# Moving twelve merge steps of a dilated attention and giving four weight slices another place

## The chip, the cores and the metric

The kernel runs on one core of a Trainium2 chip. A core has five engines with a queue of instructions each: PE (TensorE, matrix products into PSUM), DVE (VectorE), ACT (ScalarE), POOL (GpSimd) and SP (SyncE, which here issues the DMAs). They wait for each other by semaphores alone. The metric is the device time of one execution in microseconds (us).

## The reference

One decoder layer on x of 1024 rows by 1024 columns, all in float32. A single projection feeds three attention branches: A (three head groups with dilations 1, 4 and 16, merged per position by their softmax denominators), B (sliding window, eight query heads that share two key heads, with sinks) and M (four heads against 256 memory rows). Then come gates, an output projection and a feed-forward part with a short convolution. Cut to what the change touches:

```python
def dilated_mixture_attn(qkv_a, positions, q_gain, k_gain):
    for gi, (window, dil) in enumerate(A_GROUPS):
        ...
        o, lse = banded_attn(to_residue(q, dil)[:, :, None], to_residue(k, dil),
                             to_residue(v, dil), window // dil)
        outs.append(from_residue(o[:, :, 0], dil))
        lses.append(from_residue(lse[:, :, 0], dil))
    w = jax.nn.softmax(jnp.stack(lses), axis=0)
    o = jnp.einsum('gbshd,gbsh->bshd', jnp.stack(outs), w.astype(qkv_a.dtype))

def memory_attn(mq, mem, mem_gain, w_kv, q_gain, k_gain):
    ...
    q = rmsnorm(mq.reshape(b, s, M_HEADS, M_HEAD_DIM), q_gain)
    sc = jnp.einsum('bshd,bmhd->bhsm', q, mk).astype(jnp.float32) * (M_HEAD_DIM ** -0.5)
```

## The kernel before

The first part of the kernel, `input_projections`, is a chain of 44 jobs: a job projects one tile of 128 rows of the normalised input by one stage's weights. The stages are A with dilation 1 (jobs 0 to 7), the memory's keys and values (8 to 11), A with dilation 4 (12 to 19), A with dilation 16 (20 to 27), B (28 to 35) and M (36 to 43). Every job is cut into eight steps k = 0 to 7, and (j, k) is step k of job j. Each engine runs through the same double loop in its own queue; the order within a step is that in which the code is written. The attention of job j is done in the steps of job j + 2 (`LAG`): scores on PE, minima of the scores on DVE, exponentials on ACT, transposes of them on PE, products with the values on PE.

*What belongs to a projection.* q and k of job j come out of PSUM in (j+1, 0) by `normalise` on DVE (L1018, L1023, L1025), are multiplied by gains and rotated on POOL (L721 to L737), and are transposed on PE by `turn` in step 5 or 6 of job j+1 (L1345) and, for B, the key once more in step 7 (L1342). `turn` waits until POOL is done, and the second one also until ACT has copied q out of the bank (`copy_q`, L838). `sum_squares` (L999, DVE) stands at the start of the next job, in front of POOL's power (L712), on which `normalise` waits.

*The weights.* Every stage has eight slices, numbered n = 0 to 55 over all stages; those of M are 48 to 55. SP loads slice n (`load_slice`), ACT rounds it to its high part (L799, `cast_slice`), DVE subtracts (L513, `w_low`) to make the low part. The high part has one place for each k, so slice n can be cast only when the last job of the stage before has used slice n - 8. For M the casts of 48 to 52 stand in steps 2 to 6 of job 35, those of 53 to 55 at the start of job 36, in ACT's queue ahead of the copies and exponentials of (36, 0). `raw_place` says where a raw slice lies: M's slices rotate over three places of the buffer `w_raw`, and a load waits (`raw_before`) for the low part of the slice that lay there.

*The merge of A.* The outputs of the three dilations lie in rows 0 to 5 of `attn_out`, one row for each group g and pair of heads. Twelve merge steps m = 0 to 11 (`merge_use`, DVE) multiply them by factors and add them up: m // 6 is the pair of heads, (m // 2) % 3 the group, m % 2 the half. A step of group 0 is one instruction (L1156), one of group 1 or 2 is a product (L1166) and a sum (L1168). `MERGE_AT` lists the job and step of each; `merge_from` is 30. The factors come by DMA into two buffers, `load_factors(q)` for steps 2q and 2q + 1, each once the buffer's last use is over (`factor_used`).

*The late factors.* B's factors are finished in job 38: `late_gaps` (L1128) at the end of job 37, `late_factors` (L1134, L1135, DVE) in (38, 2), and `turn_late` (L1401), a transpose on PE in (38, 4), which waits for them:

```python
                if j == late_from + 1 and k == 4:
                    turn_late()
```

In the trace below job 33 begins on PE near 397.5 us, job 35 near 428.4, job 36 at 445.5, job 37 at 461.3, job 38 at 474.2 and job 39 at 484.2.

Of the kernel before, what the change touches and what calls it, by code (L numbers as in the profile page):

```python
# [68 lines left out]
def half_of(row, h):  # L69
    return 4 + 2 * row + h, 1  # L70


def whole(row):
    return 4 + 2 * row, 2
# [3 lines left out]
RAW_PLACES = ([W0, W1] + [half_of(r, h) for r in (6, 7, 8, 9) for h in range(2)] +  # L78
              [W0, W1] + [half_of(r, h) for r in (6, 7) for h in range(2)] +
              [whole(8), whole(9), W0, W1, whole(6), whole(7), W0, W1] +  # L80
              [whole(6), whole(7), W0, W1] * 4)


def raw_place(n):

    return RAW_PLACES[n - 8] if n < 48 else (n % 3, 1)


def raw_group(n):

    if n < 8:
        return 2 + n
    first = raw_place(n)[0]
    if n >= 48:
        return 7 + first
    return first // 2 if first < 4 else 2 + first - 16


def raw_before(n):

    def pieces(m):
        if m < 8:
            return set()
        first, pieces = raw_place(m)
        if m >= 48:
            return {0, 1, 2, 3}
        return set(range(first, first + pieces))

    def shared(m):
        return raw_group(m) == raw_group(n) or (pieces(m) & pieces(n) and not (m >= 48 and n >= 48))  # L110
    return next((m for m in range(n - 1, -1, -1) if shared(m)), None)


def raw_uses(n):
    return sum(raw_group(m) == raw_group(n) for m in range(n + 1))
# [50 lines left out]
def at(do, step, *more):  # L166
    if 0 <= step < len(STEPS) and STEPS[step] is not None:
        do(STEPS[step], *more)
# [64 lines left out]
def layer(nc, x, mem, positions, attn_norm, w_in, a_q_norm, a_k_norm, b_q_norm, b_k_norm, b_sinks,  # L233
# [14 lines left out]
    with ExitStack() as whole:  # L248
# [34 lines left out]
        with ExitStack() as middle:  # L283
# [26 lines left out]
            with ExitStack() as combining:  # L310
# [5 lines left out]
        ahead = Ahead(ffn_area, f_hi, plain_lo, f_in, blocks, sem("first_hi_done"), sem("first_lo_done"))  # L316

        input_projections(nc, x_t, mem_t, positions, attn_norm, w_in, a_q_norm, a_k_norm, b_q_norm,
                          b_k_norm, b_sinks, mem_norm, w_mem_kv, m_q_norm, m_k_norm, w_gate, w_raw, first_gate,
                          first_gate_in, stats_dram, factor_dram, late_dram, ps, act_hi, act_lo, ident, ident_ready, half_power, attn_out,  # L320
# [34 lines left out]
def input_projections(nc, x_t, mem_t, positions, attn_norm, w_in, a_q_norm, a_k_norm, b_q_norm, b_k_norm,  # L355
# [8 lines left out]
    with ExitStack() as ctx:  # L364
# [3 lines left out]
        def sem(name):  # L368
            return ctx.enter_context(nc.semaphore(name))
# [65 lines left out]
        group_added = sem("group_added")  # L435
# [11 lines left out]
        def x_half(n, h):  # L447
# [6 lines left out]
        last_job_of = {s: max(j for j in range(NJ) if JOBS[j][0] == s) for s in range(len(STAGES))}  # L454
        merge_from = next(j for j in range(NJ) if KIND[j] == "B") + 2

        MERGE_AT = [(merge_from + d, k) for d, k in ((2, 0), (2, 4), (3, 4), (4, 4), (5, 4), (6, 4), (7, 4),
                                                     (8, 1), (8, 5), (8, 7), (9, 1), (9, 5))]
        LATE_AT = [(merge_from + d, k) for d in (10, 11, 12, 13) for k in (2, 6)]
        late_from = last_job_of[5] + LAG  # L460

# [7 lines left out]
        def raw(n):  # L469
            if n < 8:  # L470
                return w_first[:, n, :]
            first, pieces = raw_place(n)
            if n >= 48:
                return w_raw[:].rearrange("p a n -> p (a n)")[:, 512 * first:512 * first + 512]
            if first < 4:
                return w_raw[:, first // 2, :]
            return attn_out[:, (first - 4) // 2, 512 * (first % 2):512 * (first % 2 + pieces)]
# [7 lines left out]
        def x_split(eng, n):  # L485

            even = sum(x_low_on_pool(m) for m in range(n))
            if even:
                eng.wait_ge(x_lo_pool, even)
            eng.wait_ge(x_lo_dve, n - even)  # L490
# [80 lines left out]
        def _(sp):  # L571
            def load_x(n):
                sp.dma_start(x_slot[n], x_t[n] if n < 8 else mem_t[n - 8]).then_inc(x_in[X_GROUP[n]], 16)

            def load_slice(n):
                kind, _, _, col, na, nb, _ = STAGES[n // 8]
                src = w_mem_kv if kind in ("memk", "memv") else w_in
                k = n % 8
                if raw_before(n) is not None:
                    w_split(sp, raw_before(n))  # L580
                sp.dma_start(raw(n)[:, 0:na + nb],
                             src[0, k * P:(k + 1) * P, col:col + na + nb]).then_inc(raw_in[raw_group(n)], 16)
# [22 lines left out]
            def reorder_stats():  # L605

                sp.wait_ge(exp_done, 2 * pairs_before(last_job_of[3] + 1))
                sp.dma_start(stats_dram[0].rearrange("(t p) c -> p t c", p=P), stats[:, 0]).then_inc(stats_out, 16)
                for b in range(2):
                    sp.dma_start(stats_dram[1].rearrange("(b i r) c -> b i r c", b=2, r=4)[b],  # L610
                                 stats[:, 1].rearrange("p (r b) c -> p b r c", b=2)[:, b]).then_inc(stats_out, 16)
                sp.wait_ge(stats_out, 48)
                for g in range(2):
                    sp.dma_start(stats[:, g], stats_dram[g].rearrange("(p t) c -> p t c", t=8)).then_inc(stats_in, 16)

            def store_factors():

                sp.wait_ge(factors_ready, 1)
                sp.dma_start(factor_dram.rearrange("r (p t) -> p r t", t=8),
                             merge["f"][:].rearrange("p (r t) -> p r t", t=8)).then_inc(factors_out, 16)  # L620
                sp.wait_ge(factors_out, 16)

            def load_factors(q):

                pair, g = q // 3, q % 3
                if q >= 2:
                    sp.wait_ge(factor_used, 2 * (q - 1))
                for e in range(2):
                    sp.dma_start(factor_rows[64 * e:64 * e + 64, q % 2, :],
                                 factor_dram[4 * g + 2 * pair + e].partition_broadcast(64)).then_inc(factor_in[q % 2], 16)  # L630
# [9 lines left out]
            for n in range(8, 8 * len(STAGES)):  # L640
                if n == 8 * 5:
                    reorder_stats()
                if n == 8 * 6:
                    store_factors()
                    load_factors(0)
                    load_factors(1)
                if n in (8 * 6 + 3, 8 * 6 + 5):
                    load_factors(2 if n == 8 * 6 + 3 else 3)
                if n == 8 + 2:
                    x_split(sp, 2)  # L650
                    for m in (8, 9):
                        load_x(m)
                if n in (10, 12, 14, 16):
                    x_split(sp, n // 2)
                load_slice(n)
# [271 lines left out]
        def _(dve):  # L927
# [221 lines left out]
            def merge_use(m):  # L1149

                pair, g, half = merge_batch(m)
                dve.wait_ge(factor_in[(m // 2) % 2], 32 * (m // 4 + 1))
                dst = attn_out[:, pair, half * 512:(half + 1) * 512]
                rows = factor_rows[:, (m // 2) % 2, half * 512:(half + 1) * 512]
                if g == 0:
                    dve.tensor_tensor(dst, rows, dst, ALU.mult).then_inc(factor_used, 1)  # L1156
                    dve.wait_ge(factor_used, m + 1)
                    return
                src = attn_out[:, 2 * g + pair, :]
                if g == 1:  # L1160
                    src = src.rearrange("p (r b i) -> p b i r", r=4, b=2)[:, half]
                    rows, dst = (a.rearrange("p (i r) -> p i r", r=4) for a in (rows, dst))
                else:
                    src = src.rearrange("p (t i) -> p i t", t=8)[:, half * 64:(half + 1) * 64]
                    rows, dst = (a.rearrange("p (i t) -> p i t", t=8) for a in (rows, dst))
                dve.tensor_tensor(src, rows, src, ALU.mult).then_inc(factor_used, 1)  # L1166
                dve.wait_ge(factor_used, m + 1)
                dve.tensor_tensor(dst, dst, src, ALU.add).then_inc(group_added, 1)  # L1168
                dve.wait_ge(group_added, 4 * pair + 2 * (g - 1) + half + 1)
# [18 lines left out]
            for j in range(NJ + LAG + 1):  # L1188
# [24 lines left out]
                for k in range(8):  # L1213
                    if k in step_slices(j):
# [4 lines left out]
                        at(copy_out, n - 2)  # L1219
                    if (j, k) in MERGE_AT:  # L1220
                        merge_use(MERGE_AT.index((j, k)))
                    if (j, k) in LATE_AT:
# [36 lines left out]
        def _(pe):  # L1259
# [26 lines left out]
            def project(j, part, k):  # L1286
                s, t = JOBS[j]
                kind, order, _, _, na, nb, tiles = STAGES[s]
                n = 8 * s + k
                if part == "a" and k == 0:  # L1290
# [1965 lines left out]
```

## Time and profile before

| | us |
|---|---|
| median of 3 runs (lowest, highest) | 1643.06 (1641.81, 1645.39) |
| the profiled execution, its own time | 1643.44 |
| its span, first to last instruction | 1641.5 |
| PE busy | 1604.5 |
| DVE busy | 1034.5 |
| POOL busy | 903.6 |
| ACT busy | 706.5 |

The span is what the trace covers; the execution took 1.9 us more than it. Busy times are sums over instructions. A matrix product's end is modelled, and its duration overlaps with the next one's start, so starts are compared rather than durations.

### The profile page before, as it was taken

How to read it: one execution, taken by the hardware profiler on the slowest of the kernel's cores; microseconds unless marked ns; L12 is line 12 of the kernel's file. 1: busy time of each engine (PE TensorE's matmuls, PEld its weight loads, DVE VectorE, ACT ScalarE, POOL GpSimd, SP SyncE). 2: the span in 40 equal slices, each digit the busy share in tenths (PEclk: the TensorE clock that was granted, in tenths of full speed). 3: DMA queues.
4: the chain of work that ended last, by engine and by line, in shares of the span. 5: the costliest groups of instructions: out<-in, count | busy, mean ns of one | idle time of the engine just before them, and what ended most of it. 6: DMA issues, size and time to landing. Idle time of an engine off the chain costs nothing.

```text
span 1641.5 us, 22736 instructions
## 1 busy us (share of the span) xinstructions
PE 1604.5 (98%) x8387; PEld 1322.6 (81%) x8387; DVE 1034.5 (63%) x1479; ACT 706.5 (43%) x1253; POOL 903.6 (55%) x680
## 2 busy tenths in 40 slices
PE   7999999999999999999999999999999999999999
PEld 6887878878878788888888887878888888888887
DVE  6555242345666593223655257988888888889896
ACT  5555565545554434334312223443343344454442
POOL 4643656644322297776345566989999999400000
PEclk9999999999999999999999999999999999999999
DMA  6113011002121323332555711322222222496253
GB/s 228 40 62 106 1 40 43 17 24 60 46 53 39 89 86 112 121 120 80 147 164 156 251 51 52 90 90 78 77 77 80 88 85 95 160 348 236 90 166 136
DMA packets 145865, 167.63 MB, mean 102 GB/s; under 512 B 16852, under 2 KB 97500, under 8 KB 145756
## 3 DMA queue, kind: packets, MB, share of 16 engines
q1 hardware_dynamic: 145324, 166.17, 31.5%
q8 instruction: 68, 1.11, 0.3%
q14 instruction: 41, 0.34, 0.1%
q10 hardware_dynamic: 432, 0.01, 0.0%
HBM read 133.50 MB, written 32.65 MB: 101 GB/s over the span
## 4 chain that ended last, share of the span: by engine, by line
PE 62%; POOL 2%; DVE 1%; ACT 0%; issue 0%; POOLq 0%; ACTq 0%
PE ps L3121 25%; PE ps L3222 13%; PE ps L2201 11%; PE ps L2241 7%; PE ps L2257 5%; POOL f_lo L1928 1%; PE ps L2192 1%; PE ps L2250 0%; POOL ffn_area L1940 0%; POOL ffn_area L1938 0%; POOL ffn_area L1941 0%; POOL ffn_area L1943 0%; DVE t_all L2881 0%; DVE ffn_area L2165 0%; POOL f_lo L2854 0%
## 5 line engine op out<-in xcount | busy, mean ns | idle before, releaser
L2854 POOL TENSOR_TENSOR f_lo<-ffn_area,f_hi 128x1024 fp32r<-128x1024 f32 (+1 forms) x83 | 198.9, 2416 | 20.4 <-ACT f_hi L2727 20.4
L3121 PE MATMUL ps<-t_all,f_hi 128*128 128x512 f32 x528 | 164.0, 392 | 2.0 <-DVE t_all L2881 1.6
L2727 ACT ACTIVATE f_hi<-ffn_area 128x1024 fp32r<-128x1024 f32 x85 | 80.2, 946 | 174.2 <-PE ps L3121 162.9
L3222 PE MATMUL ps<-attn_lo 128*128 128x512 f32 x624 | 143.7, 389 | 0.0
L3222 PEld LDWEIGHTS ps<-attn_lo 128*128 128x128 f32 x624 | 117.2, 188 | 24.4
L3121 PE MATMUL ps<-act_hi,f_hi 128*128 128x512 f32 x336 | 132.8, 395 | 1.3 <-POOL f_lo L2854 1.3
L1928 POOL TENSOR_TENSOR f_lo<-ffn_area,f_hi 128x1024 fp32r<-128x1024 f32 (+1 forms) x42 | 98.2, 2341 | 63.5 <-ACT f_hi L1772 63.5
L3121 PE MATMUL ps<-act_hi,f_lo 128*128 128x512 f32 x336 | 131.8, 392 | 0.0
L3121 PE MATMUL ps<-act_lo,f_hi 128*128 128x512 f32 x336 | 130.8, 389 | 0.0
L1319 PE MATMUL ps<-w_hi,act_hi 128*128 128x512 f32 (+1 forms) x320 | 121.6, 380 | 3.2 <-DVE qk L1025 1.9
L710 POOL TENSOR_SCALAR head_rstd<-head_ss 128x8 f32<-128x8 f32 (+2 forms) x42 | 10.4, 248 | 204.3 <-DVE head_ss L999 204.3
L3121 PEld LDWEIGHTS ps<-t_all,f_hi 128*128 128x128 f32 x528 | 98.9, 188 | 24.5 <-DVE t_all L2881 1.7
L1319 PE MATMUL ps<-w_lo,act_hi 128*128 128x512 f32 (+1 forms) x320 | 111.9, 350 | 0.0
L1319 PE MATMUL ps<-w_hi,act_lo 128*128 128x512 f32 (+1 forms) x320 | 111.7, 349 | 0.0
L3121 PE MATMUL ps<-t_all,f_lo 128*128 128x512 f32 x264 | 103.4, 392 | 0.0
L862 ACT ACTIVATE prob_t<-ps 128x512 f32<-128x512 f32 (+1 forms) x96 | 50.4, 525 | 121.6 <-PE ps L1423 115.4
L721 POOL TENSOR_TENSOR qk<-qk,gains 128x256 f32<-128x256 f32 (+1 forms) x74 | 62.7, 847 | 49.7 <-DVE qk L1023 30.1
L2920 DVE TENSOR_TENSOR attn_out<-attn_out 128x1024 f32<-128x1024 f32 x22 | 68.6, 3118 | 21.4 <-ACT attn_out L2782 21.4
L2257 PE MATMUL ps<-wo,act_hi 128*128 128x512 f32 x256 | 81.0, 397 | 0.0
L3121 PEld LDWEIGHTS ps<-act_hi,f_hi 128*128 128x128 f32 x336 | 63.1, 188 | 15.5 <-POOL f_lo L2854 1.7
L3121 PEld LDWEIGHTS ps<-act_hi,f_lo 128*128 128x128 f32 x336 | 63.0, 188 | 14.9
L2201 PE MATMUL ps<-t_all,f_hi 128*128 128x512 f32 x240 | 74.5, 391 | 0.0
(363 smaller groups left out, 4358.7 us busy)
## 6 DMA issues: line engine op xcount, KB each, us to landing
ffn_area<-in_w_up_dram SPq DMA_DIRECT2D x44, 512.0 KB, 5.2
gate<-gates SPq DMA_DIRECT2D x24, 512.0 KB, 3.6
ffn_area<-in_w_gate_dram SPq DMA_DIRECT2D x23, 512.0 KB, 5.1
z<-attn_out SPq DMA_DIRECT2D x22, 512.0 KB, 2.6
gates<-ffn_area SPq DMA_DIRECT2D x40, 256.0 KB, 2.1
t_raw<-in_w_down_dram SPq DMA_DIRECT2D x34, 256.0 KB, 6.4
attn_out<-in_x_dram SPq DMA_DIRECT2D x16, 512.0 KB, 6.1
f_raw<-in_w_down_dram SPq DMA_DIRECT2D x26, 256.0 KB, 4.7
```

Source lines behind the costliest of these rows:

```text
L721: ins = pool.tensor_tensor(buf[:, h0:h1, :], buf[:, h0:h1, :], gains[:, off:off + dh].unsqueeze(1).to_broadcast([P, h1 - h0, dh]), ALU.mult)
L862: act.activation(prob_t[:, u, :, c0:2, :], prob_turn[:, :, c0:2, :], ACT.Copy).then_inc(prob_copied, 1)
L1319: ins = pe.matmul(dst, lhs, w[:, k, cols], start=(k == 0 and i == 0), stop=(k == 7 and i == 2))
L1928: pool.tensor_tensor(part_place(p, part, f_lo), part_source(p, part), part_place(p, part, f_hi).bitcast(F32), ALU.subtract).then_inc(w_lo_ ...
L2201: ins = pe.matmul(gate_bank(p, i), w[:, slot, cols], a[:, k, :], start=(k == 0 and m == 0), stop=(k == 3 and m == 2))
L2241: ins = pe.matmul(o_bank(at), w[:, i0 + i, :], a[:, t0 + i, HALF[half]], start=(i == 0 and m == 0), stop=(i == tiles - 1 and m == 2))
L2257: ins = pe.matmul(ps[:, n % 4, :], a[:, k, t * P:(t + 1) * P], wo[:, slot, w, :], start=(k == 0 and i == 0), stop=(k == NK - 1 and i == 2))
L2727: act.activation(part_place(p, part, f_hi, first_hi), part_source(p, part), ACT.Copy).then_inc(w_hi_done, 1)
L2854: pool.tensor_tensor(part_place(p, part, f_lo, first_lo), part_source(p, part), part_place(p, part, f_hi, first_hi).bitcast(F32), ALU.subt ...
L2920: dve.tensor_tensor(conv[:, 0, :], conv[:, 0, :], conv[:, 1, :], ALU.mult).then_inc(z_done, 1)
L3121: ins = pe.matmul(out, w, a, start=(start and k == 0 and i == 0), stop=(stop and k == 3 and i == 2))
L3222: ins = pe.matmul(down_bank(i, t), z[a][:, t * P:(t + 1) * P], w[b], start=(k == 0 and n == 0), stop=(k == DEPTH - 1 and n == 2))
```

## The change

Two things are changed. The merge steps take other places: they stand two a job in steps 1 and 5 of jobs 32 to 35, and the last four in (37, 1), (37, 5), (37, 7) and (38, 1). Before, they stood in (32, 0), (32, 4), (33, 4), (34, 4), (35, 4), (36, 4), (37, 4), (38, 1), (38, 5), (38, 7), (39, 1) and (39, 5). And slices 51 to 54 are no longer loaded into `w_raw` but into the halves of rows 2 and 4 of `attn_out`, which hold outputs of pair 0 that are merged after step m = 5; SP waits for that (`group_added`, 4) before it loads them, and both `load_factors(2)` and `(3)` stand ahead of that wait. Slice 55 takes the first place of `w_raw`.

```diff
+LAST_PLACES = [(0, 1), (1, 1), (2, 1)] + [half_of(r, h) for r in (2, 4) for h in range(2)] + [(0, 1)]
+
 def raw_place(n):
-    return RAW_PLACES[n - 8] if n < 48 else (n % 3, 1)
+    return RAW_PLACES[n - 8] if n < 48 else LAST_PLACES[n - 48]
...
     if n >= 48:
-        return 7 + first
+        return {8: 3, 9: 5, 12: 6, 13: 4}[first] if first >= 8 else 7 + first
...
-        if m >= 48:
+        if m >= 48 and first < 4:
             return {0, 1, 2, 3}
...
-        MERGE_AT = [(merge_from + d, k) for d, k in ((2, 0), (2, 4), (3, 4), (4, 4), (5, 4), (6, 4), (7, 4),
-                                                     (8, 1), (8, 5), (8, 7), (9, 1), (9, 5))]
+        MERGE_AT = [(merge_from + d, k) for d, k in ((2, 1), (2, 5), (3, 1), (3, 5), (4, 1), (4, 5), (5, 1), (5, 5),
+                                                     (7, 1), (7, 5), (7, 7), (8, 1))]
...
-            if n >= 48:
+            if n >= 48 and first < 4:
                 return w_raw[:].rearrange("p a n -> p (a n)")[:, 512 * first:512 * first + 512]
...
-                if n in (8 * 6 + 3, 8 * 6 + 5):
-                    load_factors(2 if n == 8 * 6 + 3 else 3)
+                if n == 8 * 6 + 3:
+                    load_factors(2)
+                    load_factors(3)
+                    sp.wait_ge(group_added, 4)
```

SP's queue from the loads of slices 48 to 50 on, before. `factor_rows` are the merge factors, `w_raw<-in_w_in_dram 128x512` is a slice of M:

```order
L581 DMA w_raw<-in_w_in_dram 128x512 [waits w_lo_dve,w_lo_pool] x3
L629 DMA factor_rows<-factors 64x1024 [waits factor_used]
L629 DMA factor_rows<-factors 64x1024
L581 DMA w_raw<-in_w_in_dram 128x512 [waits w_lo_dve,w_lo_pool] x2
L629 DMA factor_rows<-factors 64x1024 [waits factor_used]
L629 DMA factor_rows<-factors 64x1024
L581 DMA w_raw<-in_w_in_dram 128x512 [waits w_lo_dve,w_lo_pool] x3
```

The same place of the changed kernel:

```order
L584 DMA w_raw<-in_w_in_dram 128x512 [waits w_lo_dve,w_lo_pool] x3
L632 DMA factor_rows<-factors 64x1024 [waits factor_used]
L632 DMA factor_rows<-factors 64x1024
L632 DMA factor_rows<-factors 64x1024 [waits factor_used]
L632 DMA factor_rows<-factors 64x1024
L584 DMA attn_out<-in_w_in_dram 128x512 [waits w_lo_dve,w_lo_pool,group_added]
L584 DMA attn_out<-in_w_in_dram 128x512 [waits w_lo_dve,w_lo_pool] x3
L584 DMA w_raw<-in_w_in_dram 128x512 [waits w_lo_dve,w_lo_pool]
```

Slices 51 to 54 come in one run behind a wait for the merge, into `attn_out`; only slice 55 still goes to `w_raw`.

DVE's queue from (37, 5) to `late_factors` in (38, 2), before. `late` is what `late_gaps` and `late_factors` work on, `small<-ps` the minima of M's scores:

```order
L1156 TENSOR_TENSOR attn_out<-factor_rows,attn_out 128x512
L1128 TENSOR_TENSOR late<-late,neg_sink 128x64
L999 TENSOR_REDUCE head_ss<-square 128x4
L1023 TENSOR_TENSOR qk<-ps,head_rstd 128x512
L1058 TENSOR_REDUCE small<-ps 128x4
L1093 COPY attn_out<-ps 128x2x128
L1156 TENSOR_TENSOR attn_out<-factor_rows,attn_out 128x512
L1134 TENSOR_TENSOR late<-late 128x64
L1135 RECIPROCAL late<-late 128x8x8
```

The changed kernel, from the sum that ends merge step 9 (lines are 5 higher):

```order
L1173 TENSOR_TENSOR attn_out<-attn_out 128x512
L1171 TENSOR_TENSOR attn_out<-factor_rows,attn_out 128x64x8
L1173 TENSOR_TENSOR attn_out<-attn_out 128x512
L1133 TENSOR_TENSOR late<-late,neg_sink 128x64
L1004 TENSOR_REDUCE head_ss<-square 128x4
L1028 TENSOR_TENSOR qk<-ps,head_rstd 128x512
L1063 TENSOR_REDUCE small<-ps 128x4
L1098 COPY attn_out<-ps 128x2x128
L1171 TENSOR_TENSOR attn_out<-factor_rows,attn_out 128x64x8
L1173 TENSOR_TENSOR attn_out<-attn_out 128x512
L1139 TENSOR_TENSOR late<-late 128x64
L1140 RECIPROCAL late<-late 128x8x8
```

Ahead of the reciprocal of `late` there stand now three merge steps of a product and a sum (9, 10 and 11; the product of 9 is the row ahead of those shown), where two single products stood (6 and 7).

DVE's queue in job 33, steps 0 and 1, before, from the copy of an output (`attn_out<-ps`) through `normalise` (`qk<-ps,head_rstd`) to the first minima of step 4:

```order
L1093 COPY attn_out<-ps 128x2x128
L1018 TENSOR_TENSOR qk<-ps,head_rstd 128x2x4x64
L1025 TENSOR_TENSOR qk<-ps,head_rstd 128x128
L1069 ISA prob,late<-ps,masks,neg_sink 128x256
L1069 ISA late 128x1
L1069 ISA prob,late<-ps,masks,neg_sink 128x256
L1069 ISA late 128x1
```

The changed kernel:

```order
L1098 COPY attn_out<-ps 128x2x128
L1023 TENSOR_TENSOR qk<-ps,head_rstd 128x2x4x64
L1030 TENSOR_TENSOR qk<-ps,head_rstd 128x128
L1171 TENSOR_TENSOR attn_out<-factor_rows,attn_out 128x128x4
L1173 TENSOR_TENSOR attn_out<-attn_out 128x512
L1074 ISA prob,late<-ps,masks,neg_sink 128x256
L1074 ISA late 128x1
```

Merge step 2 has moved from behind those minima to right behind `normalise`; in job 34 step 4 has moved in the same way.

## Rows read from the trace of the kernel before

**Rows 1.** The page: busy time, share of the span and instructions of each engine.

```profile
PE 1604.5 (98%) x8387; PEld 1322.6 (81%) x8387; DVE 1034.5 (63%) x1479; ACT 706.5 (43%) x1253; POOL 903.6 (55%) x680
```

**Rows 2.** Busy time by stretch: us, then each engine, clock, DMA share, GB/s.

```profile
450.00:500.00 50.00, 47.63 (x335) 38.37 (x334) 33.87 (x73) 25.18 (x72) 12.14 (x18) 1.00 0.20 53
```

**Rows 3.** Timeline of the SP queue: start, us, engine, line, operation, out<-in, count.

```profile
445.01 2.27 SPq L581 DMA_DIRECT2D w_raw<-in_w_in_dram  x3
```

**Rows 4.** Timeline of ACT, same columns; in brackets idle before it and releaser.

```profile
447.76 0.63 ACT L799 ACTIVATE w_hi<-w_raw 128x512 fp32r<-128x512 f32 x1 [0.65 <-DMA w_raw<-in_w_in_dram]
450.22 1.27 ACT L799 ACTIVATE w_hi<-w_raw 128x512 fp32r<-128x512 f32 x2 [1.82 <-DMA w_raw<-in_w_in_dram]
451.39 0.58 ACT L862 ACTIVATE prob_t<-ps 128x512 f32<-128x512 f32 x1
```

**Rows 5.** Timeline of PE in job 36.

```profile
450.60 0.40 PE L1319 MATMUL ps<-w_hi,act_lo 128*128 128x512 f32 x1
452.12 0.63 PE L1392 MATMUL ps<-ident,prob 128*128 128x128 f32 x4 [1.12 <-ACT prob_t L862]
...
453.74 0.39 PE L1319 MATMUL ps<-w_hi,act_lo 128*128 128x512 f32 x1
454.85 0.63 PE L1392 MATMUL ps<-ident,prob 128*128 128x128 f32 x4 [0.73 <-ACT prob_t L862]
...
458.37 0.60 PE L1345 MATMUL ps<-ident,qk 128*128 128x128 f32 x4
...
460.42 0.39 PE L1319 MATMUL ps<-w_hi,act_lo 128*128 128x512 f32 x1
461.17 0.30 PE L1342 MATMUL ps<-ident,qk 128*128 128x128 f32 x1 [0.36 <-issue]
```

**Rows 6.** Timeline of POOL in job 36: gain multiply and end of the rotation.

```profile
453.55 1.82 POOL L721 TENSOR_TENSOR qk<-qk,gains 128x512 f32<-128x512 f32 x2 [3.41 <-DVE qk L1025]
...
456.92 0.52 POOL L737 TENSOR_TENSOR qk<-rope_a,rope_b 128x160 f32<-128x160 f32 x1
```

**Rows 7.** Timeline of DVE in jobs 37 to 39.

```profile
472.38 0.68 DVE L1156 TENSOR_TENSOR attn_out<-factor_rows,attn_out 128x512 f32<-128x512 f32 x1
...
475.64 0.69 DVE L999 TENSOR_REDUCE head_ss<-square 128x4 f32<-128x512 f32 x1 [1.16 <-ACT square L808]
...
479.81 0.68 DVE L1156 TENSOR_TENSOR attn_out<-factor_rows,attn_out 128x512 f32<-128x512 f32 x1
480.53 0.22 DVE L1134 TENSOR_TENSOR late<-late 128x64 f32<-128x64 f32 x1
480.78 0.56 DVE L1135 RECIPROCAL late<-late 128x64 f32<-128x64 f32 x1
...
485.85 1.04 DVE L1166 TENSOR_TENSOR attn_out<-factor_rows,attn_out 128x512 f32<-128x512 f32 x1
...
488.02 0.69 DVE L999 TENSOR_REDUCE head_ss<-square 128x4 f32<-128x512 f32 x1
```

**Rows 8.** Timeline of PE in job 38, at the transpose of the late factors.

```profile
481.31 0.39 PE L1319 MATMUL ps<-w_hi,act_lo 128*128 128x512 f32 x1
481.53 0.27 PE L1401 MATMUL ps<-ident,late 128*64 128x128 f32 x1
```

**Rows 9.** Timeline of DVE: a subtraction in stage one, a minimum in job 33.

```profile
42.92 1.22 DVE L499 TENSOR_TENSOR act_lo<-attn_out,act_hi 128x1024 fp32r<-128x1024 f32 x1
...
407.79 0.48 DVE L1069 CUSTOM_DVE_ANT_1 prob<-ps,masks,neg_sink 128x256 f32<-128x256 f32 x1 [3.83 <-PE ps L1378]
```

**Rows 10.** Timeline of POOL: rotations in stage one and in job 33.

```profile
43.01 1.45 POOL L732 TENSOR_TENSOR rope_a<-qk,rope_cos 128x128 f32<-128x128 f32 x1
...
55.06 0.46 POOL L732 TENSOR_TENSOR rope_a<-qk,rope_cos 128x128 f32<-128x128 f32 x1
...
407.42 0.52 POOL L737 TENSOR_TENSOR qk<-rope_a,rope_b 128x160 f32<-128x160 f32 x1
```

**Rows 11.** Timeline of PE: the transpose of q and k in job 33.

```profile
409.91 0.60 PE L1345 MATMUL ps<-ident,qk 128*128 128x128 f32 x4
```

## The prediction

> **What bounds the kernel now.** I read the page first: PE is busy 1604.5 of 1641.5 us [rows 1], so only what PE waits can be won, and whatever makes it wait is lost. The change touches the stretch of jobs 32 to 39, so the table by stretch comes next: from 450 to 500 us PE is busy 47.63 of 50 us at a granted clock of 1.00 [rows 2], which leaves 2.4 us. Idle time in the records is a lower bound, because modelled ends overlap; in the timeline the reader should compare starts. Two products of 512 columns start 0.22 us apart [rows 8], so a gap above 0.23 behind one is a stall.
>
> In job 36 [rows 5] shows three of them. 450.60 to 452.12 is 1.52 instead of 0.23: 1.29 us of stall, released by ACT's copy. 453.74 to 454.85 gives 0.88 in the same way, again behind ACT's copy. 460.42 to 461.17 gives 0.52, in front of the transpose of B's last key. The first two go back to a DMA. ACT's last two casts start at 450.22 after 1.82 us of waiting for `w_raw`, and the copy that PE needs stands behind them, at 451.39 [rows 4]. SP could issue the last three slices only from 445.01 on, each when a place was free [rows 3]. PE went on 0.15 after the copy's end (451.39 + 0.58 to 452.12), which I take as the delay of a semaphore.
>
> **The change, part by part.**
>
> *The four slices.* Slices 51 to 54 are loaded once merge step 5 is done, in (34, 5), more than a job ahead of their use, and slice 55 waits only for the low part of slice 48, where before the run of [rows 3] waited for those of 50 to 52. All are in before the casts at the start of job 36. ACT then casts three slices on end from 447.1 (447.76 less its wait of 0.65, [rows 4]): the pair at 450.22 took 1.17 to the next start, 0.59 each [rows 4], so 1.75 for three, and the copy starts near 448.9 instead of 451.39. Its end at 449.5 is before 450.83 (450.60 + 0.23), where PE wants it. The exponentials and the second copy follow at the pace of DVE's minima and end, by my estimate, near 452.2, before PE's 452.7 (454.85 - 2.17). Both stalls go: -2.17 us at (36, 4).
>
> *What is late next.* The first transpose for job 35 was at 458.37 [rows 5]; it would be wanted at 456.20. It needs POOL, whose rotation ends at 456.92 + 0.52 = 457.44 [rows 6]. POOL started at 453.55 behind `normalise`, which stands on DVE behind the minima that follow PE's scores of (36, 0), ahead of both stalls, and three subtractions; nothing there is moved by the change. With 0.13 for the semaphore PE goes on at 457.57, so 1.37 of the 2.17 come back as a wait for POOL and 0.80 are left. The third stall of 0.52 was a wait for ACT's copy of q, which stood behind exponentials that are now 2.17 earlier, while PE gets there only 0.80 earlier: it goes. (If that copy keeps PE waiting anyway, 0.5 less.) In sum job 37 starts 0.80 + 0.52 = 1.3 us earlier. Bounds: 0.8, when the third stall stays, and 2.7 (1.29 + 0.88 + 0.52), when POOL isn't in the way.
>
> *The last four merge steps.* They now stand ahead of `late_factors`, for which PE waits in (38, 4). I keep times relative to PE's place, as in the trace before. A step of product and sum takes 488.02 - 485.85 = 2.17 us [rows 7]. Step 8 in (37, 1) fits into DVE's idle time before the minima. From 472.38, where one product of 0.68 stood, the queue is now: step 9 to 474.55, step 10 to 476.72, `late_gaps` (0.25, like the start distance from 480.53 to 480.78) to 476.97. Then `sum_squares`, POOL's power, `normalise`, minima and copy, which took 479.81 - 475.64 = 4.17 from the first to the place of the next merge step: 481.14. DVE's idle 1.16 ahead of 475.64 is used up on the way. Step 11 to 483.31, `late_factors` 0.81 (480.53 to 480.78 + 0.56): 484.12. With 0.15 for the semaphore PE gets it at 484.27 [rows 7]. PE wanted it at 481.53 and had it with 0.19 to spare, with no idle time shown [rows 8]. So PE stalls 2.7 us there. Behind it stand the rest of the projection of job 38 and everything after; nothing gives it back, because PE in the M jobs has hardly a gap to fill. Bounds: 2.2, if part of the chain from `sum_squares` overlaps, and 3.6, if step 8 runs into the minima of (37, 4) and one product more is slowed.
>
> *Merge steps beside POOL.* In jobs 33 and 34 a step of 2.17 us now starts right behind `normalise`, when POOL multiplies and rotates. DVE has room: it was idle 3.83 us before the minima at 407.79 [rows 9]. POOL may not have. A rotation's product that began at 43.01 under DVE's subtraction of two SBUF operands (42.92, 1.22 long) took 1.45 us, the same at 55.06 took 0.46 [rows 9, 10]: 0.99 more, 80% of the other's length. In job 33 POOL ends at 407.42 + 0.52 = 407.94 [rows 10] and PE transposes at 409.91 [rows 11], so it has 1.97 less 0.15. 80% of 2.17 is 1.74: just no stall. All of it would be 0.35 us. I take 0.1 for each of two jobs, bounds 0 and 0.5 each. Job 35's step is one product of 0.68 and hidden; step 0 only goes behind `normalise` instead of in front.
> The Trainium skill (SBUF — State Buffer, on the shared GpSimd/Vector port) says that the port pair is an exclusive lock: of a DVE instruction with two SBUF inputs and a GpSimd instruction that reads SBUF, the second one waits until the first has ended. By that rule a job would lose the 0.35 us, two jobs 0.7 instead of 0.2, and the total below would be +2.1 instead of +1.6; the 0.99 of rows 10 agrees with it in kind.
>
> *The rest costs nothing.* Steps 6 and 7 in job 35 stand ahead of `w_low` of slices that ACT has yet to cast. Freed DVE time in (36, 4) and jobs 38 and 39 lay in no gap of PE. SP's loads of factors 4 and 5 come some 20 us before use; if they were late, step 8 would wait and all behind it.
>
> *Sum.* -1.3 + 2.7 + 0.2 = +1.6 us. The profiled execution took 1643.44, 0.4 above the median, and would become 1645.0; against the median of 1643.06 that is **1644.7 us**, +0.10%. What can be told from no change here is about 0.2%, 3.3 us: 1639.8 to 1646.3.
>
> **The rivals.**
>
> 1. *The wait on the late factors doesn't come* (0.14), because the chain is shorter than I add up. For it: the 4.17 holds a wait for POOL's power that may overlap. Against it: PE had 0.19 to spare and three times 2.17 replaces twice 0.68. Time: -1.3 + 0.2, 1642.0.
>
> 2. *The wait on the late factors is longer* (0.16). Mechanism: merge steps are products and sums of two SBUF operands, each can be held by POOL (step 8 by the gain multiply, step 11 by that of job 37), and what they lose adds up in one queue ahead of the reciprocal. The cost decides at 4.5 us instead of 2.7, that is with the reciprocal's end 1.8 later, past 485.9 in the old frame. With 5 us: -1.3 + 5 + 0.2, 1647.0, slower. For it: an instruction in rows 10 was stretched by 0.99, and two such would do. Against it: POOL is idle for the whole of steps 9 and 10.
>
> 3. *POOL isn't in the way in job 36 and both gains come whole, with no late wait* (0.04): -2.7, or -3.5 with what else is idle in rows 2: 1639.6 to 1640.4, about the bound of faster.
>
> 4. *The change doesn't do what it says* (0.06): slices 51 to 54 wait, since SP is held by factor loads or the merge wait, and ACT waits as before. No gain and the loss stays: +2.9, 1646.0.
>
> **How the numbers follow.** The forecast's own case has 0.60, with bounds -2.7 + 2.2 = -0.5 to -0.8 + 3.6 + 1.0 = +3.8 at its ends. Its upper tail past 3.3 is 0.03, and rivals 2 and 4 add 0.12 and 0.02 to slower; rival 3 and a lucky draw of rival 1 give 0.05 to faster. A median of three moves by about 1 us. The range of 8 in 10 runs from rival 1 less 1 us to rival 2 (1641.0 to 1647.2).
>
> **What would show it.** Right: ACT's casts of slices 53 to 55 in one run near 447.1 without a DMA wait; the transpose of (36, 5) with an idle time released by POOL L737; job 37 starting near 460.0; PE idle for 2 to 3 us in front of the transpose of `late`, released by the reciprocal on DVE; later jobs unchanged. Wrong: DVE reaching the reciprocal before 482, new gaps of PE in jobs 33 or 34 above 0.5 us, or a shift that arises behind job 39.

## The result, and the profile after

Over 20 runs each, the changed kernel took 1645.86 us in the median (1643.42 to 1648.14) and the one before 1643.42 (1641.57 to 1646.84). The ratio is 1.0015, 95% interval 1.0008 to 1.0021: 2.5 us slower, between 1.3 and 3.5. The profiled execution's span is 1643.0 us, 1.5 more than before. The prediction's 1644.7 (+0.10%) has the sign and lies 1.2 below the median.

The page after: PE's busy time is 1604.1 us against 1604.5 ([rows 1]), so its idle time within the span is 38.9 against 37.0. The granted clock doesn't show in this comparison, because each of the two executions has one stretch at the lower clock, as the tables below show.

```profile
PE 1604.1 (98%) x8387; PEld 1321.9 (80%) x8387; DVE 1038.7 (63%) x1479; ACT 707.0 (43%) x1253; POOL 906.0 (55%) x680
```

SP after, in the columns of the timelines of before: the loads of slices 51 to 54 in one run behind merge step 5, and slice 55 alone.

```profile
426.53 1.76 SPq L584 DMA_DIRECT2D attn_out<-in_w_in_dram  x4
437.08 0.33 SPq L584 DMA_DIRECT2D w_raw<-in_w_in_dram  x1
```

ACT after, at the start of job 36. Where [rows 4] has two waits for the DMA, the casts of slices 53 to 55 stand end to end:

```profile
445.78 1.14 ACT L804 ACTIVATE w_hi<-attn_out 128x512 fp32r<-128x512 f32 x2
446.82 0.62 ACT L804 ACTIVATE w_hi<-w_raw 128x512 fp32r<-128x512 f32 x1
448.31 0.60 ACT L867 ACTIVATE prob_t<-ps 128x512 f32<-128x512 f32 x1 [0.88 <-PE ps L1428]
```

PE after in job 36, and POOL's last instruction of that rotation:

```profile
449.64 0.60 PE L1397 MATMUL ps<-ident,prob 128*128 128x128 f32 x4
...
451.23 0.39 PE L1324 MATMUL ps<-w_hi,act_lo 128*128 128x512 f32 x1
451.79 0.63 PE L1397 MATMUL ps<-ident,prob 128*128 128x128 f32 x4 [0.17 <-ACT prob_t L867]
...
455.08 0.40 PE L1324 MATMUL ps<-w_hi,act_lo 128*128 128x512 f32 x1
456.20 0.66 PE L1350 MATMUL ps<-ident,qk 128*128 128x128 f32 x4 [0.72 <-POOL qk L742]
...
458.53 0.27 PE L1347 MATMUL ps<-ident,qk 128*128 128x128 f32 x1
```

```profile
455.62 0.52 POOL L742 TENSOR_TENSOR qk<-rope_a,rope_b 128x160 f32<-128x160 f32 x1
```

Against [rows 5] the first gap is gone (no idle time at 449.64) and the second is down from 0.73 to 0.17 us of idle time, by starts from 0.88 to 0.33 (451.23 to 451.79, less 0.23). At 456.20 stands what [rows 5] didn't have: 0.72 us idle, by starts 0.89, ended by POOL, whose rotation ends at 456.14. At 458.53 there is no wait. To measure a stretch in spite of what lies ahead of it, I take the distance between two marks of PE. From the transpose of B's last key but one (445.23 before, 444.00 after) to that of the last (461.17 and 458.53) it is 15.94 us before and 14.53 after: 1.41 us gained. I call this distance that of job 36.

DVE after, from the first of the moved merge steps in (37, 5) to the reciprocal of the late factors:

```profile
469.74 1.08 DVE L1171 TENSOR_TENSOR attn_out<-factor_rows,attn_out 128x512 f32<-128x512 f32 x1
...
472.00 1.10 DVE L1171 TENSOR_TENSOR attn_out<-factor_rows,attn_out 128x512 f32<-128x512 f32 x1
...
474.23 0.22 DVE L1133 TENSOR_TENSOR late<-late,neg_sink 128x64 f32<-128x64 f32 x1
474.37 0.68 DVE L1004 TENSOR_REDUCE head_ss<-square 128x4 f32<-128x512 f32 x1
...
478.53 1.04 DVE L1171 TENSOR_TENSOR attn_out<-factor_rows,attn_out 128x512 f32<-128x512 f32 x1
...
480.68 0.23 DVE L1139 TENSOR_TENSOR late<-late 128x64 f32<-128x64 f32 x1
480.94 0.56 DVE L1140 RECIPROCAL late<-late 128x64 f32<-128x64 f32 x1
```

Steps 9 and 10 take 2.26 and 2.23 us, `sum_squares` to the next merge step 4.16 (4.17 in [rows 7]), step 11 2.15. PE, at the transpose of the late factors and behind it:

```profile
478.59 0.39 PE L1324 MATMUL ps<-w_hi,act_lo 128*128 128x512 f32 x1
481.55 0.30 PE L1406 MATMUL ps<-ident,late 128*64 128x128 f32 x1 [2.58 <-DVE late L1140]
...
481.93 0.63 PE L1324 MATMUL ps<-w_lo,act_hi 128*128 128x512 f32 x1
482.36 0.63 PE L1324 MATMUL ps<-w_hi,act_lo 128*128 128x512 f32 x1
...
485.33 0.39 PE L1324 MATMUL ps<-w_lo,act_hi 128*128 128x512 f32 x1
```

PE stood idle for 2.58 us until DVE's reciprocal, where [rows 8] has no wait. Then a second thing is to be seen, of which the prediction said nothing: the products of 512 columns behind the wait start 0.43 us apart (481.93, 482.36) and only from 485.33 on 0.23 again. The table by stretch says why; its columns are us, PE, PEld, DVE, ACT, POOL, clock, DMA share, GB/s:

```profile
480.00:484.00 4.00, 2.45 (x7) 1.87 (x8) 2.98 (x9) 1.02 (x3) 0.00 (x0) 0.74 0.00 0
484.00:486.00 2.00, 2.00 (x9) 1.75 (x8) 0.00 (x0) 0.61 (x2) 0.00 (x0) 0.67 0.07 16
486.00:490.00 4.00, 4.00 (x28) 3.24 (x28) 1.79 (x3) 0.59 (x1) 1.72 (x3) 1.00 0.97 231
```

The granted clock fell from 1.00 to 0.74 and 0.67, from 2.4 GHz to 1.2 GHz for a part of the stretch, right behind the wait. From the transpose of the last key to that of the late factors it is 20.36 us before and 23.02 after: 2.66 lost. From there to the product from which on all spacings are equal again it is 2.18 us before (481.53 to 483.71, the row of before below) and 3.78 after (481.55 to 485.33), 1.6 more; some 20 us on, 1.5 of them are left.

```profile
483.71 0.40 PE L1319 MATMUL ps<-w_lo,act_hi 128*128 128x512 f32 x1
```

In jobs 33 and 34 PE lost nothing. POOL's two gain multiplies in job 33, its last instruction, and DVE's merge step beside it:

```profile
402.80 2.08 POOL L726 TENSOR_TENSOR qk<-qk,gains 128x512 f32<-128x512 f32 x1 [2.39 <-DVE qk L1030]
404.96 1.17 POOL L726 TENSOR_TENSOR qk<-qk,gains 128x128 f32<-128x128 f32 x1
...
407.68 0.54 POOL L742 TENSOR_TENSOR qk<-rope_a,rope_b 128x160 f32<-128x160 f32 x1
```

```profile
402.64 1.09 DVE L1171 TENSOR_TENSOR attn_out<-factor_rows,attn_out 128x512 f32<-128x512 f32 x1
403.76 2.04 DVE L1173 TENSOR_TENSOR attn_out<-attn_out 128x512 f32<-128x512 f32 x1
```

The two gain multiplies took 3.33 us in all, where 1.8 is usual ([rows 6]: 1.82; alone they are 1.29 and 0.47 in job 33 before), and the step's sum 2.04 instead of 1.1. POOL was done at 408.22 and PE's transpose came at 408.78 without a wait.

So the profiled execution's 1.5 us are: -1.41 in job 36, +2.66 in the wait, +1.5 in the clock, and -1.2 near 340 us, where the two kernels' programs are still alike, so that the change can't be the cause. There PE waits 1.9 to 2.0 us for POOL in both executions, and the clock fell behind it before but not after:

```profile
340.00:345.00 5.00, 5.00 (x24) 4.29 (x22) 1.24 (x2) 1.43 (x4) 0.88 (x2) 0.69 0.01 3
```

```profile
340.00:345.00 5.00, 5.00 (x39) 4.08 (x38) 1.25 (x2) 1.76 (x5) 2.12 (x2) 1.00 0.01 3
```

Without that the difference would be +2.7 us, and the medians say +2.5.

### The profile page after: what moved, and what is told of

Read it like the earlier page. It is cut to its first block, busy times and chain, and to the rows that moved or that the text cites. A ratio compares the mean times of both kernels' runs of the same rounds, so it can differ in the third digit from the quotient of the medians.

```text
span 1643.0 us, 22734 instructions
## 1 busy us (share of the span) xinstructions
PE 1604.1 (98%) x8387; PEld 1321.9 (80%) x8387; DVE 1038.7 (63%) x1479; ACT 707.0 (43%) x1253; POOL 906.0 (55%) x680
## 4 chain that ended last, share of the span: by engine, by line
PE 62%; POOL 2%; DVE 1%; ACT 0%; issue 0%; POOLq 0%; ACTq 0%
PE ps L3126 25%; PE ps L3227 13%; PE ps L2206 11%; PE ps L2246 7%; PE ps L2262 5%; POOL f_lo L1933 1%; PE ps L2197 1%; PE ps L2255 0%; POOL ffn_area L1945 0%; POOL ffn_area L1943 0%; POOL ffn_area L1946 0%; POOL ffn_area L1948 0%; DVE t_all L2886 0%; DVE ffn_area L2170 0%; POOL f_lo L2859 0%
## 5 line engine op out<-in xcount | busy, mean ns | idle before, releaser
L726 POOL TENSOR_TENSOR qk<-qk,gains 128x256 f32<-128x256 f32 (+1 forms) x74 | 67.0, 905 | 48.9 <-DVE qk L1028 30.1
```

Of the source, the lines that this page charges most:

```text
L726: ins = pool.tensor_tensor(buf[:, h0:h1, :], buf[:, h0:h1, :], gains[:, off:off + dh].unsqueeze(1).to_broadcast([P, h1 - h0, dh]), ALU.mult)
```

## The experiments

Two questions were open. Is the loss the wait for the late factors with the clock behind it (my theory), or do the merge steps beside POOL or the slices' places cost it? And is the gain in job 36 that of the slices, or of the earlier merge steps? Each kernel had 11 timed runs and one profile; e1 to e4 are compared with the same 33 runs of before, e5 to e7 with the same 27.

**e1: the last four merge steps back.**

```diff
-                                                     (7, 1), (7, 5), (7, 7), (8, 1))]
+                                                     (8, 5), (8, 7), (9, 1), (9, 5))]
```

> The changed kernel with the last four merge steps back where they were, in (38, 5), (38, 7), (39, 1) and (39, 5); the eight early steps and the slices stay changed. My theory: the whole loss is PE's wait for the reciprocal of the late factors in (38, 4) (2.6 us idle in the profile after) and the lower clock behind it (products 0.43 instead of 0.23 us apart until 485.3 us, about 1.4 us). Here no idle time before the transpose of the late factors, job 37 still 1.4 us earlier: 1.4 us faster than before, ratio 0.999, and about 4 us faster than the changed kernel. Rival: the loss comes from the merge steps beside POOL in jobs 33 and 34 or from the slices in attn_out: then it stays 2 to 3 us slower than before.

Measured: 1642.01 us, ratio 0.9994 (0.9985 to 1.0003) to before. Since the changed kernel stands at 1.0008 to 1.0021, the intervals don't meet: the loss is in the last four steps. Its size fits the expectation (3.9 us below the changed kernel's median, about 4 expected). PE at the transpose of the late factors, and the clock behind it:

```profile
479.28 0.27 PE L1406 MATMUL ps<-ident,late 128*64 128x128 f32 x1
```

```profile
478.00:483.00 5.00, 5.00 (x28) 4.09 (x27) 3.63 (x8) 3.21 (x9) 0.00 (x0) 1.00 0.00 0
```

No wait and the clock at 1.00. Job 36 between the two marks took 14.52 us, as after. That the kernel is faster than before by 1.4 us lies inside the interval and isn't shown by the medians; the trace shows it for job 36, and from there to the transpose of the late factors 20.27 us against 20.36, so nothing is lost again.

**e2: only the last merge step behind the late factors.**

```diff
-                                                     (7, 1), (7, 5), (7, 7), (8, 1))]
+                                                     (7, 1), (7, 5), (7, 7), (8, 5))]
```

> The changed kernel with only the last merge step behind the late factors, in (38, 5) instead of (38, 1). My theory: the chain in front of the reciprocal is 2.15 us shorter, so PE waits 0.5 us instead of 2.7; whether the clock falls behind a wait that short decides between -0.9 us against before (clock stays at 2.4 GHz) and about +0.4 (it falls as in the profile after). Rival: the length of the DVE chain is not what PE waits for: the wait stays near 2.6 us and the time 2 to 3 us above before.

Measured: 1642.69 us, ratio 0.9996 (0.9987 to 1.0005).

```profile
480.51 0.30 PE L1406 MATMUL ps<-ident,late 128*64 128x128 f32 x1 [0.41 <-DVE late L1140]
```

```profile
478.00:483.00 5.00, 4.59 (x26) 3.49 (x25) 3.63 (x10) 3.05 (x11) 1.28 (x1) 1.00 0.00 0
```

One step of 2.15 us fewer ahead of the reciprocal, and the wait is 0.41 us instead of 2.58. The wait goes by the length of DVE's chain, one for one. Behind this wait the clock stayed. By the distances the kernel should be 1.0 us below before (1.44 gained in job 36, 0.48 lost behind it), as I had said for a clock that stays; the interval holds this and no change at all.

**e3: slices 51 to 54 back in `w_raw`.**

```diff
-LAST_PLACES = [(0, 1), (1, 1), (2, 1)] + [half_of(r, h) for r in (2, 4) for h in range(2)] + [(0, 1)]
+LAST_PLACES = [(n % 3, 1) for n in range(48, 56)]
...
-                    sp.wait_ge(group_added, 4)
```

> The changed kernel with slices 51 to 54 back in the three places of w_raw, without SP's wait for the merge (both factor loads stay ahead of slice 51). My theory: the gain in job 36 is due to the slices alone, so ACT waits for the DMA again at the start of job 36, PE has its 1.3 and 0.9 us there, and the late wait of 2.7 us with the lower clock behind it stays: 4 us slower than before in all, ratio 1.0024. Rival: the earlier merge steps free DVE in (36, 4) and that is the gain: then it runs as the changed kernel, +2.4.

Measured: 1646.02 us, ratio 1.0017 (1.0008 to 1.0026). I had said 1.0024, and the interval holds both that and the rival's figure, so the time doesn't decide. The trace does, and it gives neither theory its full due. ACT at the start of job 36:

```profile
448.58 0.63 ACT L803 ACTIVATE w_hi<-w_raw 128x512 fp32r<-128x512 f32 x1 [0.56 <-DMA w_raw<-in_w_in_dram]
450.13 0.63 ACT L803 ACTIVATE w_hi<-w_raw 128x512 fp32r<-128x512 f32 x1 [0.92 <-DMA w_raw<-in_w_in_dram]
451.22 0.63 ACT L803 ACTIVATE w_hi<-w_raw 128x512 fp32r<-128x512 f32 x1 [0.46 <-DMA w_raw<-in_w_in_dram]
```

ACT waits for the DMA again, three times, and PE behind it. Still job 36 took 15.39 us between the marks: 0.55 less than before, 0.86 more than after. The 0.55 us come without the slices' new places. It is tempting to give them to the order of SP's queue, where the load of slice 53 stood behind `load_factors(3)` before. The trace of before says no: those factors were issued by 440.2, and slice 53 at 445.01 [rows 3], right behind the low part of slice 50, which is what its load waits for:

```profile
444.24 0.69 DVE L513 TENSOR_TENSOR w_lo<-w_raw,w_hi 128x512 fp32r<-128x512 f32 x1 [0.17 <-ACT w_hi L799]
```

What differs is the transfer of slice 54. From issue to landing it took 4.3 us before and 2.8 in e3, though it was issued later against the first mark (1.15 us instead of 0.71). Why it was slower before is open; nothing here tells an effect of the change from chance.

**e5: eight merge steps early, slices in `w_raw`, last four steps late.**

```diff
-LAST_PLACES = [(0, 1), (1, 1), (2, 1)] + [half_of(r, h) for r in (2, 4) for h in range(2)] + [(0, 1)]
+LAST_PLACES = [(n % 3, 1) for n in range(48, 56)]
...
-                                                     (7, 1), (7, 5), (7, 7), (8, 1))]
+                                                     (8, 5), (8, 7), (9, 1), (9, 5))]
...
-                    sp.wait_ge(group_added, 4)
```

> As e1 (last four merge steps late), and slices 51 to 54 back in w_raw: eight merge steps early and nothing else. With no late wait in it, this tells what the slices' places give by themselves. In e3 job 36 was 0.55 us shorter than before instead of 1.41, with ACT still waiting for the DMA. My theory: job 36 again 0.5 us shorter than before and 0.9 longer than e1; total 0.5 us below before. Rival: with the late wait away the slices' places give the whole 1.4 us, and this runs as before.

Measured: 1643.57 us, ratio 0.9999 (0.9990 to 1.0008). Job 36 took 14.91 us between the marks, from 447.76 to 462.67: 1.03 less than before, 0.39 more than e1. The rival (as before, 15.94) is wrong in this trace; my 0.5 us below before was too little, and 0.9 above e1 too much. e3 and e5 differ by 0.48 us in a stretch where their programs are alike: the transfer of slice 55, the last one that ACT waits for, took 3.3 us in e3 and 2.8 in e5. So the places are worth 0.86 us in one pair of traces (e3 against after) and 0.39 in the other (e5 against e1), and this difference follows how long the last transfer took; the whole gain against before is 1.41. With the new places ACT waits for no transfer there, and job 36 is the same in every trace: 14.50 to 14.54 us in after, e1, e2, e6 and e7, against 15.94, 15.39 and 14.91 in before, e3 and e5. That the earlier merge steps give any part of the gain is shown by none of them.

**e6: PE kept at work while it waits.**

```diff
-                pe.wait_ge(factors_ready, 2)
                 pe.wait_ge(sq_done, count(QK_KINDS, last_job_of[5] + 1))
...
+                for _ in range(24):
+                    pe.transpose(ps[:, PB, 0:P], ident[:], ident[:])
+                pe.wait_ge(factors_ready, 2)
```

> The changed kernel with 24 transposes of the identity on PE just before it waits for the late factors, into the PSUM bank that the wait's transpose overwrites; they take about 2.1 us of the 2.6 us in which PE had been idle. My theory: PE waits as long as before (0.4 us idle at most are left), but the granted clock stays at 2.4 GHz behind it: products 0.23 us apart, 1.4 us faster than the changed kernel. Rival: the lower clock from 481.6 us on has another cause (it came at 340 us in the trace of before): then it comes here too, and the time is that of the changed kernel.

**e7: the changed kernel once more.**

> The changed kernel once more, on the same chip and in the same call as the two others. Ratio to before 1.0015. If the lower clock belongs to the late wait, products are 0.43 us apart behind it again; at 340 us, behind another wait of PE of 1.9 to 2.0 us, it may fall or not, as it did in before but not in after.

Measured side by side: e6 1644.21 us, ratio 1.0007 (0.9999 to 1.0016); e7 1646.86 us, ratio 1.0022 (1.0013 to 1.0030). PE in e7 and in e6:

```profile
482.06 0.30 PE L1406 MATMUL ps<-ident,late 128*64 128x128 f32 x1 [2.59 <-DVE late L1140]
...
483.02 0.63 PE L1324 MATMUL ps<-w_hi,act_hi 128*128 128x512 f32 x1
483.45 0.63 PE L1324 MATMUL ps<-w_lo,act_hi 128*128 128x512 f32 x1
```

```profile
478.80 2.78 PE L1406 MATMUL ps<-ident 128*128 128x128 f32 x24
481.62 0.30 PE L1408 MATMUL ps<-ident,late 128*64 128x128 f32 x1
...
481.99 0.39 PE L1324 MATMUL ps<-w_lo,act_hi 128*128 128x512 f32 x1
482.21 0.40 PE L1324 MATMUL ps<-w_hi,act_lo 128*128 128x512 f32 x1
```

In e7 the wait is 2.59 us, and from 483.02 on products are 0.43 us apart. In e6 24 transposes fill 478.80 to 481.58 (2.78 us, where I had expected 2.1), the wait ends at the same place in the program 2.8 us after PE got there, and the products behind it stay 0.23 apart. The stretch from 480 to 487 us, first in e7 and then in e6:

```profile
480.00:487.00 7.00, 4.94 (x17) 4.00 (x18) 3.45 (x10) 2.59 (x7) 0.00 (x0) 0.76 0.07 12
```

```profile
480.00:487.00 7.00, 6.97 (x44) 5.89 (x43) 3.72 (x10) 2.20 (x5) 1.03 (x2) 1.00 0.11 29
```

The kernels differ in whether PE had work while it waited. One trace of each could be chance, as near 340 us, but the mean granted clock of every run is on record too, and by my estimate a halved clock for 3.3 of 1643 us makes it 0.001 lower. It is 0.998 in six runs of e7 and 0.999 in the other five; in e6 it is 0.999 in six and 1.000 in five. So the low clock is a consequence of the idle time. It costs 1.6 us in these two traces (from the late factors' transpose to the transposes of (39, 1) 5.63 us, 482.06 to 487.69, against 4.04, 481.62 to 485.66). The medians differ by 2.65 us, with intervals that overlap a little; the 1 us beyond the traces' 1.6 is not explained. Without the low clock the sum of the distances is -1.40 + 2.76 = +1.4 us for e6, and its ratio says +1.2.

**e4: `normalise` ahead of the three subtractions.** On top of e1:

```diff
                     if k in step_slices(j):
                         n = steps_before(j) + step_slices(j).index(k)
                         at(minima, n)
-                        for m in released(j - 1, 7) if lows_behind and k == 0 else []:
-                            w_low(dve, m)
                         at(copy_out, n - 2)
...
                     if k == 0 and 0 in step_slices(j) and 0 <= j - 1 < NJ:
                         normalise(j - 1)
+                    for m in released(j - 1, 7) if lows_behind and k == 0 else []:
+                        w_low(dve, m)
```

> As e1, and DVE does normalise in (36, 0) ahead of the three subtractions for slices 53 to 55 instead of behind them. POOL starts 1.9 us earlier. If POOL and DVE didn't hinder each other, its rotation would end 1.9 us earlier, the wait of 0.7 us before the transpose in (36, 5) would go, and the time be 0.7 us below e1. By what job 33 showed after the change (POOL's two gain multiplies took 3.33 us instead of 1.84 beside a merge step) POOL loses some 1.5 us to the three subtractions: 0.3 to 0.4 us below e1 only, with the multiplies near 3.3 us.

Measured: 1641.40 us, ratio 0.9988 (0.9979 to 0.9997): 2 us faster than before, with the lowest median of all. POOL and DVE beside each other, and PE:

```profile
450.49 2.52 POOL L726 TENSOR_TENSOR qk<-qk,gains 128x512 f32<-128x512 f32 x2 [1.54 <-DVE qk L1030]
453.09 0.85 POOL L737 TENSOR_TENSOR rope_a<-qk,rope_cos 128x160 f32<-128x160 f32 x1
...
454.88 0.53 POOL L742 TENSOR_TENSOR qk<-rope_a,rope_b 128x160 f32<-128x160 f32 x1
```

```profile
450.32 2.37 DVE L516 TENSOR_TENSOR w_lo<-attn_out,w_hi 128x512 fp32r<-128x512 f32 x2
452.62 0.94 DVE L516 TENSOR_TENSOR w_lo<-w_raw,w_hi 128x512 fp32r<-128x512 f32 x1
```

```profile
455.47 0.66 PE L1350 MATMUL ps<-ident,qk 128*128 128x128 f32 x4
...
458.12 0.30 PE L1347 MATMUL ps<-ident,qk 128*128 128x128 f32 x1 [0.16 <-issue]
```

POOL lost 0.7 us in the multiplies (2.52 against 1.80) and 0.3 in the next product (0.85 against 0.52), and DVE's three subtractions took 3.2 us instead of 1.9: each held the other. The transpose at 455.47 has no wait for POOL any more. Job 36 took 14.10 us between the marks, 0.42 less than e1. That is the expected 0.3 to 0.4, but partly by luck: POOL lost 1.05 us and not 1.5, so that the first transpose came 0.74 earlier, and 0.32 of that came back at the second (0.16 idle at 458.12). The bracket there names no other engine; ACT's copy of q, for which this transpose waits, ends at 458.02. This explanation is from the trace; the intervals of e4 and e1 overlap.

## Why the prediction was right, and where it fell short

*The three stalls of job 36.* The gain of 1.3 us was 1.41: 0.94 up to the transpose of (36, 5), where I had 0.80, and 0.47 behind it for 0.52. The way to it had an error that cost nothing. I had the first copy on ACT start when the casts end; it waits for PE's products with the values as well (idle 0.88 at 448.31, released by PE), so it came later and 0.33 us by starts stayed at (36, 4), where I had both stalls gone. As POOL was the later of the two anyway, the wait for POOL was only so much shorter (0.89 instead of 1.37). That what comes next is POOL's rotation, with a wait in front of (36, 5), is what the trace shows, and e4 took it away.

*The wait for the late factors.* 2.7 predicted, 2.66 measured, by the chain as it was added up (2.26, 2.23, 4.16 and 2.15 us for terms of 2.17, 2.17, 4.17 and 2.17, and 0.14 for the 0.25 of `late_gaps`, which evened out the steps' excess). e1 and e2 show that PE waits for the length of this chain.

*The term that was missing.* The step that fell short is "so PE stalls 2.7 us there. Behind it stand the rest of the projection of job 38 and everything after": I priced the wait as idle time alone. In all three executions profiled with that wait (after, e3, e7) the clock fell behind it, for 1.5 to 1.6 us more. With it the sum is -1.4 + 2.7 + 1.5 = +2.8 us, 1646.2 against the measured 1645.86. The forecast of +1.6 came near the measured +2.5 although 1.5 us of cost were missing, because the rest erred by 0.3 the other way (the gain 0.1 too small, 0.2 for the steps beside POOL that cost nothing) and the wait alone is larger than the gain. The trace of before had a hint that I did not read: near 340 us PE waited 2.0 us and the clock was 0.69 in the stretch behind.

*The merge steps beside POOL.* 0.1 us for each of two jobs; there was none. POOL lost 1.51 us in job 33, not 1.74, and had 1.82 to lose. The rows show turns: POOL's first multiply, issued at 402.80 under DVE's product, ended 1.15 us behind the product's end (403.73); DVE's sum, issued at 403.76, ended 0.92 behind that multiply (404.88); and POOL's second multiply, issued at 404.96, ended 0.33 behind the sum (405.80). Alone these three take 1.29, 1.10 and 0.47 us, so each ended 0.14 to 0.18 us less than its own length behind the end of the one that held it. The pair in [rows 9] and [rows 10] gives the same: the product ended 0.32 behind the subtraction, and takes 0.46 alone. So the 80% of the prediction was a wait for what was left of one instruction, and not a share that holds for any overlap. The Trainium skill's rule (SBUF — State Buffer, section "SBUF: two separate sides"), that whichever starts first holds the pair for the whole instruction and the other waits, agrees with all four. The 0.35 us a job that the prediction drew from it did not come, because POOL waits only for what is left of an instruction and not for both in full.

*The rivals.* 1 is out: the wait came. 2 (a wait of 4.5 us or more) is out: the wait was 2.66, and steps 9 and 10 met no POOL instruction; but the clock put the price part of the way to where that rival would have gone. 3 is out by the wait for POOL. 4 is out: the slices had landed when ACT cast them.

## What to carry to other kernels

Work that is moved out of one wait lands ahead of another: before a list of steps is moved on an engine, add up what then stands in front of each result that a full engine needs, here a small transpose with 0.19 us to spare. Price a wait of the matrix engine of some 2 us and more with what its clock may lose behind it (here 1.2 us near 340 us and 1.6 behind the wait), and where the wait can't be removed, keep the engine busy with transposes that nobody reads. When a gap is closed, look which engine is next: only 1.4 of the 2.7 us were to be had until POOL got its input earlier, and 1.8 after that.

## What was not expected of the hardware

The granted clock fell to 1.2 GHz behind an idle time of PE of 2.6 us in all three profiled executions that had one (after, e3, e7), not behind 0.41 us (e2), and not when transposes filled the time (e6). Near 340 us, in the same place of the program, PE waited 1.9 to 2.9 us for POOL in all nine traces, and the clock fell in before, e2, e3 and e5 (idle 2.00, 1.89, 2.87 and 2.04 us) but not in after, e1, e4, e6 and e7 (1.90 to 1.92). These two places are the only ones in the nine traces.

The mean granted clock of a run counts such falls. Of the profiled executions it is 1.000 in those without a fall (e1, e4, e6), 0.999 with one (before, after, e2, e5, e7) and 0.998 with two (e3). By it no run of the changed kernel was without a fall (20 of after, 11 of e7), while 15 of the 33 runs of before that e1 to e4 are compared with were. But 4 of e3's 11 runs show 1.000 as well, so if the wait is as long in them as in the profiled one (2.56 us), the fall does not always come behind it. The falls go with the time: of the 20 runs of the changed kernel the eleven at 0.999 have a median of 1644.94 us, the six at 0.998 1647.01 and the three at 0.997 1647.91. This is a good part of why runs of one kernel differ by up to 5 us, though not all of it: the runs at 0.999 alone spread over 2.8 us.
